# Down projections of three feed-forward layers: five seven-product pairs in place of four, and their shared sums folded earlier

## What is computed

```python
def _swiglu(t, w_gate, w_up, w_down):
    return (jax.nn.silu(t @ w_gate) * (t @ w_up)) @ w_down

for l in range(DEPTH):
    f = _swiglu(_rmsnorm(h, ffn1_pre_g[l]), ffn1_w_gate[l], ffn1_w_up[l], ffn1_w_down[l])
    h = h + 0.5 * _rmsnorm(f, ffn1_post_g[l])
    ...
    f = _swiglu(_rmsnorm(h, ffn2_pre_g[l]), ffn2_w_gate[l], ffn2_w_up[l], ffn2_w_down[l])
    h = h + 0.5 * _rmsnorm(f, ffn2_post_g[l])
```

## Time and profile before

| | |
|---|---|
| median of 3 runs (lowest, highest) | 1839.95 us (1839.8, 1840.28) |
| the profiled execution, its own time | 1839.19 us |
| its span, first to last instruction | 1837.2 us |
| TensorE busy | 1822.0 us (99%) |
| VectorE busy | 1372.0 us (75%) |
| ScalarE busy | 1115.8 us (61%) |
| GpSimd busy | 222.5 us (12%) |
| chain that ended last | PE 94%, DVE 4%, ACT 1%, issue 1% |
| HBM read | 330.91 MB, 181 GB/s over the span |
| granted TensorE clock, mean | 0.999 |

### The profile page before, as it was taken

How to read it: one execution, slowest core, us unless ns; L and a number is a source line. 1 busy time by engine, 2 the same in 40 slices (tenths; PEclk the granted TensorE clock), 3 DMA queues, 4 the chain that set the end, 5 groups by cost and what they waited for, 6 DMA issues and landing times.

```text
span 1837.2 us, 29020 instructions
## 1 busy us (share of the span) xinstructions
PE 1822.0 (99%) x10909; PEld 1625.8 (88%) x10909; DVE 1372.0 (75%) x2184; ACT 1115.8 (61%) x1924; POOL 222.5 (12%) x170
## 2 busy tenths in 40 slices
PE   9999999999999999999999999999999999999998
PEld 7888999998888878888999888887889998989997
DVE  7775757787787888878777778878768765768764
ACT  7664554556666566656555657665557654757653
POOL 0220001110033003300111102310002210001210
PEclk9999999999999999999999999999999999999999
DMA  8775575455576557655654548655747655537652
GB/s 247 216 217 183 172 194 163 146 154 186 172 226 185 182 166 225 191 177 160 192 173 142 194 147 230 185 176 168 218 138 218 188 196 155 169 115 205 202 191 103
DMA packets 436042, 333.88 MB, mean 182 GB/s; under 512 B 25402, under 2 KB 381504, under 8 KB 435904
## 3 DMA queue, kind: packets, MB, share of 16 engines
q1 hardware_dynamic: 435440, 331.57, 59.5%
q10 hardware_dynamic: 464, 0.47, 0.1%
HBM read 330.91 MB, written 1.05 MB: 181 GB/s over the span
## 4 chain that ended last, share of the span: by engine, by line
PE 94%; DVE 4%; ACT 1%; issue 1%; DMA 0%; SPq 0%; DVEq 0%; ACTq 0%
PE bank L1982 16%; PE bank L1959 14%; PE bank L1961 14%; PE bank L1960 14%; PE bank L1970 7%; PE bank L1984 7%; PE bank L1971 7%; PE bank L1972 7%; PE bank L1988 2%; DVE wlo L1250 1%; PE bank L1981 1%; DVE wsum L1383 1%; PE bank L2324 0%; PE bank L2390 0%; PE bank L2395 0%
## 5 line engine op out<-in xcount | busy, mean ns | idle before, releaser
L1250 DVE TENSOR_TENSOR wlo<-raw,whi 128x1024 fp32r<-128x1024 f32 (+3 forms) x634 | 748.7, 1189 | 224.5 <-ACT whi L676 217.8
L676 ACT ACTIVATE whi<-raw 128x1024 fp32r<-128x1024 f32 (+3 forms) x634 | 636.6, 1014 | 282.0 <-PE bank L1961 198.9
L1982 PE MATMUL bank<-U,whi 128*128 128x512 f32 x1280 | 439.1, 395 | 0.0
L1984 PE MATMUL bank<-U,wlo 128*128 128x256 f32 x1120 | 314.5, 281 | 0.0
L1970 PE MATMUL bank<-U,whi 128*128 128x256 f32 x1024 | 289.1, 282 | 0.0
L1972 PE MATMUL bank<-U,wlo 128*128 128x256 f32 x1024 | 285.9, 279 | 0.0
L1971 PE MATMUL bank<-U,whi 128*128 128x256 f32 x1024 | 285.9, 279 | 0.0
L1982 PEld LDWEIGHTS bank<-U,whi 128*128 128x128 f32 x1280 | 230.2, 188 | 42.5 <-issue 0.2
L1959 PE MATMUL bank<-whi,U 128*128 128x384 f32 (+2 forms) x592 | 218.9, 370 | 0.1
L1984 PEld LDWEIGHTS bank<-U,wlo 128*128 128x128 f32 x1120 | 210.1, 188 | 6.9
L1961 PE MATMUL bank<-wlo,U 128*128 128x384 f32 (+2 forms) x592 | 211.1, 357 | 0.0
(11 more groups left out here) (334 smaller groups left out, 2571.7 us busy)
## 6 DMA issues: line engine op xcount, KB each, us to landing
raw<-in_ffn_w_up SPq DMA_DIRECT2D x351, 256.0 KB, 3.5
raw<-in_ffn_w_down SPq DMA_DIRECT2D x264, 256.0 KB, 2.9
raw<-in_ffn_w_gate SPq DMA_DIRECT2D x175, 256.0 KB, 3.4
raw<-in_w_gate SPq DMA_DIRECT2D x128, 192.0 KB, 2.9
raw<-in_w_in SPq DMA_DIRECT2D x80, 256.0 KB, 3.4
raw<-in_a_w_in SPq DMA_DIRECT2D x48, 256.0 KB, 3.2
raw<-in_w_mem_kv SPq DMA_DIRECT2D x32, 256.0 KB, 3.2
raw<-in_w_out SPq DMA_DIRECT2D x32, 256.0 KB, 3.1
```

Of the source, the lines that this page charges most:

```text
L676: act.activation(whi[n % SLOTS][:, 0:w], unsplit(n, w), ACT.Copy).then_inc(hi_ready, 1)
L1250: dve.tensor_tensor(wlo[n % SLOTS][:, 0:w], unsplit(n, w), whi[n % SLOTS][:, 0:w].bitcast(F32), ALU.subtract).then_inc(lo_ready, 1)
L1982: ins = pe.matmul(dst, wh, u2[:, k, :], start=(k == 0), stop=(k == KT - 1))
L1984: pe.matmul(dst[:, 0:TOK], wl, uhi[:, k, :], start=False, stop=False)
```

## The change

- SEVEN becomes (1, 2, 3, 5, 6): the order of the pairs is 8 7 7 7 8 7 7 8 8, tail. One more pair of each of the three layers takes seven products.
- One of the four sums of activations (a21 + a22) is no longer kept in `ahi`, `alo`, but over the block a21 of `hhi`, `hlo`, which a seven-product pair does not read. ScalarE and GpSimd write it with an instruction of its own (128 columns, and 384 for the other three), after GpSimd has made `hlo` of that tile.
- The fold moves ahead of the last two ordinary pairs and takes nine steps: ScalarE copies bank 0 to `wsum`, VectorE forms the four shared sums between splits of the tail's chunks (bank 1 to the shared sum first, then banks 3 and 2 to that one, then bank 3 again), and adds them to banks 4 to 7 one after the other, each when TensorE has finished that bank's last matmul of the chunk before the tail (`rows_full`, new).

```diff
-SEVEN = (2, 4, 6, 8)
+SEVEN = (1, 2, 3, 5, 6)
...
-                    ahi, alo = sb("ahi", [P, NS, 4, P], F32R, m), sb("alo", [P, NS, 4, P], F32R, m)
+                    ahi, alo = sb("ahi", [P, NS, 3, P], F32R, m), sb("alo", [P, NS, 3, P], F32R, m)
...
         def _(pool):
...
-                        pool.wait_ge(ahi_done, x + 1)
-                        pool.tensor_tensor(alo[:, x % NS, :, :], asum[:, :, :], ahi[:, x % NS, :, :].bitcast(F32), ALU.subtract)\
-                            .then_inc(alo_done, 1)
+                        pool.wait_ge(asum_split, 4 * x + 2)
+                        pool.wait_ge(clo_done, wide(f, n - 2) + 1)
+                        pool.tensor_tensor(hlo[:, n - 2, ts[1]], asum[:, 0, :], hhi[:, n - 2, ts[1]].bitcast(F32), ALU.subtract)\
+                            .then_inc(asum_split, 1)
+                        pool.tensor_tensor(alo[:, x % NS, :, :], asum[:, 1:4, :], ahi[:, x % NS, :, :].bitcast(F32), ALU.subtract)\
+                            .then_inc(asum_split, 1)
...
         def _(act):
...
                         act.wait_ge(asum_done, 4 * x + 4)
-                        act.activation(ahi[:, x % NS, :, :], asum[:, :, :], ACT.Copy).then_inc(ahi_done, 1)
+                        act.wait_ge(clo_done, wide(f, n - 2) + 1)
+                        act.activation(hhi[:, n - 2, ts[1]], asum[:, 0, :], ACT.Copy).then_inc(asum_split, 1)
+                        act.activation(ahi[:, x % NS, :, :], asum[:, 1:4, :], ACT.Copy).then_inc(asum_split, 1)
...
+                if f:
+                    e = ck.seven[seven_of(f, SEVEN[-1])]
+                    split_to(e + 6)
+                    act.wait_ge(lo_ready, halves_done(e + 3))
+                    act.wait_ge(w_used, e + 1)
+                    act.activation(wsum[:, 0, :], bank[0][:, :], ACT.Copy).then_inc(folded, 1)
                 split_to(n0 + ffn_chunks(f) - TAIL - 1 + SLOTS)
...
             def fold(f):
...
-                split_to(e + 5)
-                dve.wait_ge(w_used, e + 1)
-                dve.wait_ge(lo_ready, halves_done(e + 3))
-                dve.tensor_copy(wsum[:, 0, :], bank[0][:, :]).then_inc(folded, 1)
-                split_to(e + 6)
-                dve.wait_ge(w_used, e + 2)
+                last = c_down[f][-1] - 3
+                split_to(e + 9)
+                dve.wait_ge(w_used, e + 4)
                 dve.wait_ge(folded, done + 1)
-                into_bank(4, 0)
-                split_to(e + 7)
-                dve.wait_ge(w_used, e + 3)
-                add_bank(2, 2, 0)
-                add_bank(1, 3, 0)
-                dve.wait_ge(w_used, e + 4)
+                add_bank(1, 1, 0)
+                split_to(e + 10)
+                dve.wait_ge(folded, done + 2)
+                add_bank(3, 3, 1)
+                add_bank(2, 2, 1)
+                split_to(e + 11)
                 dve.wait_ge(folded, done + 4)
-                add_bank(1, 1, 1)
-                dve.wait_ge(folded, done + 5)
-                into_bank(5, 1)
-                add_bank(2, 1, 2)
-                dve.wait_ge(folded, done + 7)
-                into_bank(6, 2)
-                add_bank(3, 3, 2)
-                dve.wait_ge(folded, done + 9)
-                into_bank(7, 3)
+                add_bank(1, 3, 2)
+                for n, x in enumerate((0, 3, 2, 1)):
+                    if n < 3:
+                        dve.wait_ge(rows_full, 3 * (f - 1) + n + 1)
+                    else:
+                        dve.wait_ge(w_used, last + 1)
+                        dve.wait_ge(folded, done + 5)
+                    into_bank(4 + n, x)
...
                 def hidden_sum(n):
-                    return ahi[:, x % NS, n, :], alo[:, x % NS, n, :]
+                    if n == 0:
+                        return hhi[:, even, ts[1]], hlo[:, even, ts[1]]
+                    return ahi[:, x % NS, n - 1, :], alo[:, x % NS, n - 1, :]
...
-                                ins = down_rows(c, t, nb, 4, hhi, hlo, k, k == 0, k == FT - TAIL - 3 and t + nb == 2)
+                                ins = down_rows(c, t, nb, 4, hhi, hlo, k, k == 0, k == FT - TAIL - 1)
+                                if k == FT - TAIL - 1 and t + nb < 2:
+                                    ins.then_inc(rows_full, 1)
...
-                    pe.wait_ge(folded, 10 * (f - 1) + (2, 6, 8, 10)[2 * t + nb])
+                    pe.wait_ge(folded, 9 * (f - 1) + 6 + 2 * t + nb)
```

More of the change, by code:

```diff
@@ L294, in program @@
             sem(n) for n in ("fx_rows", "f_step", "c_full", "c_ready", "c_pair"))
-        wsum_done, asum_done, ahi_done, alo_done, folded = (
-            sem(n) for n in ("wsum_done", "asum_done", "ahi_done", "alo_done", "folded"))
+        wsum_done, asum_done, asum_split, rows_full, folded = (
+            sem(n) for n in ("wsum_done", "asum_done", "asum_split", "rows_full", "folded"))
         feat_done, gt0_full, gate_done = sem("feat_done"), sem("gt0_full"), sem("gate_done")
@@ L1232, in weight_sums @@
                     dve.wait_ge(lo_ready, halves_done(ck.seven[x - 1] + 3))
-                    dve.wait_ge(folded, 10 * (x // NS))
+                    dve.wait_ge(folded, 9 * (x // NS))
                 at = ck.slot(e) * CW
@@ L1366, in hidden_sums @@
                 if x:
-                    dve.wait_ge(alo_done, x)
+                    dve.wait_ge(asum_split, 4 * x)
                 dve.tensor_tensor(asum[:, 0, :], a21, a22, ALU.add).then_inc(asum_done, 1)
@@ L1376, in fold @@
                 e = ck.seven[seven_of(f, SEVEN[-1])]
-                done = 10 * (f - 1)
+                done = 9 * (f - 1)
                 def into_bank(n, x):
@@ L2180, in seven_products @@
                 start_chunk(o)
-                product(4, hhi[:, odd, ts[0]], hlo[:, odd, ts[0]], o, half[1], False, stop)
-                pe.wait_ge(alo_done, x + 1)
-                product(5, *hidden_sum(3), o, half[0], False, stop).then_inc(w_used, 1)
+                product(4, hhi[:, odd, ts[0]], hlo[:, odd, ts[0]], o, half[1], False, False)
+                pe.wait_ge(asum_split, 4 * x + 4)
+                product(5, *hidden_sum(3), o, half[0], False, False).then_inc(w_used, 1)
                 start_chunk(sums)
@@ L2188, in seven_products @@
                 product(1, *hidden_sum(1), ends, half[0], start, stop)
-                product(6, hhi[:, odd, ts[1]], hlo[:, odd, ts[1]], ends, half[1], False, stop).then_inc(w_used, 1)
+                product(6, hhi[:, odd, ts[1]], hlo[:, odd, ts[1]], ends, half[1], False, False).then_inc(w_used, 1)
             def down_by_seven(f, b):
```

## The result

The changed kernel takes 1844.22 us (median of 20 runs, 1839.68 to 1847.96), the kernel before beside it 1839.83 us (20 runs, 1839.11 to 1841.33): ratio 1.0023, interval 1.0017 to 1.003. It is slower by 4.4 us. The forecast was 1839.4, with a range up to 1843.5. The single runs are spread over 8 us, those of before over 2.

What follows compares the result with a forecast made beforehand. TensorE, busy in 99% of the span, bounds the kernel; VectorE's queue sets the tail's start. Tail start 48.05 plus 8.4 gives 56.45 us a layer, 169.3 for three against 169.84, 0.5 less: 1839.4 us, range 1834.5 to 1843.5.

Steps and rivals of the forecast that it cites:

- (a): Gate tiles' end: pair 1's sums delay the last multiplication 1.55 us; VectorE begins pair 2 5.45 us after down projection's first matmul.
- the 0.42: Gate tiles: extra us for pair 1's sums, as one VectorE addition takes 1.11 instead of 0.69 beside GpSimd's instruction.
- the 0.8 more that the prediction kept open: Gate tiles: estimated extra us per layer if a sum waits for all 1.21 us of GpSimd's instruction; 1841.8 in all.
- (b): Pairs 2 and 3: VectorE's split of pair 3's o comes late, stalling TensorE 0.8 to 1.0 us.
- (c): Pairs 5 and 6: VectorE's split of pair 6's o comes late, stalling TensorE another 0.4 to 0.6 us.
- (d): Last splits: VectorE waits 1.2 us for the first tail chunk, splitting it 39.85 us after down projection's first matmul.
- (e): Tail splits and shared sums: 4.54 and 2.6 us of VectorE, late loads 0.15 us a layer, between 0 and 1.1.
- The rule of the page: Tail loads: HBM to SBUF bound by about 358 GB/s a core, chunks every 1.46 us, tail start 47.9 to 48.2.
- T0 + 48.05: Forecast tail start in each layer, in us from TensorE's first matmul of the down projection (T0).
- The covers: Gate tiles: extra ScalarE, GpSimd instructions and activation sums cost nothing; a failed cover costs its length three times, 1 to 3 us.
- the raw ring decides, slower: Tail: last four chunks' loads share DMA engines and land late; slower by over 3.7 us from 4.3; chance 0.14.
- Full gain: Down projections: with VectorE's queue 2.4 us shorter per layer TensorE never waits, 7.8 us less, 1832.1; chance 0.08.

Runs made afterwards that it cites:

- Experiment 2: Changed kernel with the loads of the tail's four chunks cut to 32 of each 512 columns, so mostly stale weights: 1834.75 us, ratio 0.9973.
- experiment 1: Changed kernel with four spaced seven-product pairs, SEVEN = (1, 2, 4, 6), in place of five, new fold kept: 1832.86 us, ratio 0.9962.
- experiment 3: Changed kernel with eight more matmuls into bank 0, result unread, ahead of each tail to fill TensorE's wait: 1841.45 us, ratio 1.001.
- experiment 8: Kernel of experiment 1 with three unused VectorE additions ahead of the addition to bank 4, making TensorE wait: 1838.28 us, ratio 0.9995.
- Experiments 6: Kernel before with only the activations' sum moved over the spent block of hhi and hlo, old pairs and fold: 1839.24 us, ratio 0.9997.
- experiment 7: Kernel before with the moved activations' sum and a fifth, spaced pair, SEVEN = (1, 2, 4, 6, 8), old fold: 1837.96 us, ratio 0.9989.
- experiments 4: Kernel of experiment 1 with five unused VectorE additions ahead of the addition to bank 4, making TensorE wait: 1846.48 us, ratio 1.0034.
- experiment 5: Changed kernel with four seven-product pairs standing together right ahead of the new fold, SEVEN = (3, 4, 5, 6): 1845.29 us, ratio 1.0042.

## Why the prediction was wrong

The mechanism was the one forecast: VectorE's queue, with the fold at its end, sets the start of the tail. The price of its last stretch was too low, and what TensorE's wait itself brings was not in it.

- **(a) Start of the queue: right.** VectorE begins pair 2 at T0 + 5.2, against 5.45. The last multiplication of the gate tiles comes at 607.26, against 605.35 in the earlier trace rows; T0 itself lies 0.66 later in this execution, so the delay is 1.25 us, against 1.55. One of pair 1's sums (L1250 at 601.99) takes 1.11 us beside GpSimd's instruction, the most in the trace, so the 0.42 stood, and the 0.8 more that the prediction kept open did not come: GpSimd's instruction (601.36 to 602.56) had 0.57 us left when the sum began.
- **(b), (c) Stalls at o: right in place, the first one 0.2 us smaller.** Forecast were 0.8 to 1.0 and 0.4 to 0.6 us. The idle times are 0.39 and 0.21; by the starts TensorE loses 0.66 and 0.48. (At pair 3 the starts are 0.79 apart instead of 0.23, and the next 0.33.) The queue was 0.25 us early, so o's split in pair 3 ends at T0 + 16.2 and not 16.46. Experiment 2 has these stalls alone: its stretch of 54.98 us is 1.2 longer than experiment 1's less the 0.68 of its three matmuls.
- **(d) First tail chunk: right.** T0 + 39.64 against 39.85, with its wait of 1.18 us against 1.2.
- **(e) The step that failed.** The term for the loads was 0.15 us a layer, between bounds of 0 and 1.1; it measured 1.8 (1.51 + 0.28) in ffn(1), 1.25 in ffn(2) and 1.55 in ffn(3). The upper bound took the longest landing of the earlier trace rows, 4.0 us, as if it held for any load. But those loads come in ones and twos, and the four chunks ask for 2.1 MB in 3.8 us. The trace of before holds better rows outside the 41 us of the earlier trace rows. Its eight loads from 862.0 us on (four of 256 KB, four of 172) are such a burst, and the last lands after 5.3 us; over the whole span the loads of this line land after 2.2, 3.2 and 7.5 us (shortest, median, longest). And 334 GB/s is not its busiest stretch: 346 to 348 us has 390.

```profile
L408 SPq DMA_DIRECT2D raw<-in_w_in x8: 328/434/507, 862.0 to 865.4; - x8
...
DMA to landing us min/median/max: 2.3/3.4/5.3
```

```profile
346.00:348.00 2.00, 2.00 (x13) 2.00 (x12) 1.44 (x2) 0.98 (x3) 0.11 (x1) 1.00 1.06 390
```

  The demand was worked out (460 GB/s), and also that at 334 GB/s the fourth chunk is 1.3 us late, of which the additions between the splits cover 1.0. But the working asked only about the fourth chunk, and had the chunks come evenly. By the high parts' ends (644.54, 647.28, 649.39, 650.80) against an undisturbed queue (a split at 644.57, 645.71, 647.5 and 649.8) the second is 1.6 us late, the third 1.9 and the fourth 1.0. Ahead of the second there is no addition to cover anything, and it lands 2.7 us behind the first. While its last half was under way (641.5 to 646.2) all the later ones were issued and up to six transfers were under way at once. Over three layers the tail starts are late by 3.8 us.
- **The rule of the page.** The Trainium skill, "DMA: Bandwidth & Descriptors", section "Where 436 GB/s comes from", has about 358 GB/s from HBM to SBUF for a core. The trace goes over it for 2 us (375 GB/s, in before 390) and stays under it over the whole burst (306). It is no ceiling here, and no rate to plan with either; the measurement decides.
- **What was not in the sum.** TensorE's wait of 2.1 to 2.6 us ahead of the tail lets its clock fall in part of the executions, 1.6 us in ffn(2) of the profiled one, an estimated 2 to 2.8 us in the median (experiment 3). The forecast put the sum together as if a stall cost only its length. With the tail at T0 + 48.05 it would probably have held: TensorE would have waited 1.3 us, and with waits of 1.0 to 1.9 only two of ten runs had a lower mean clock (experiment 8). That is argued and not shown.
- **The covers: right.** Experiments 6 and 7: no cost in the gate tiles.
- **The rivals.** What came true is *the raw ring decides, slower*, which had 0.14. It said that from a landing of 4.3 us on the change is slower, and 1844.5 at 4.6; the median of the eight was 4.6 and the result 1844.2. That this fits so closely is partly chance, since the clock's share was not in it. Its chance was set by the 4.0 us of the earlier trace rows. That was no evidence against it, since the stretch has no burst in it, and the rest of the trace of before, with the burst at 862 us and its landing of 5.3, spoke for it. The prediction had named landings after 4 us and more as a sign of being wrong, and this sign came. *Full gain*, 1832.1, is what experiment 1 comes near (1832.86), with four pairs.

Four spaced pairs under the new fold, 1832.86 us, are the best kernel here. A fifth costs VectorE 4.3 us a layer, for 0.68 us of TensorE, and in experiment 1 VectorE's idle time behind pair 6 is 1.24 + 0.87 + 0.33 + 0.42 = 2.9 us. In the old fold it paid: there the tail starts at T0 + 46.02 in experiment 7, before the fold is through.

What stays open: why the rate falls from 337 to 238 GB/s between 643 and 646 us, with up to six transfers under way, and is 375 later; and what decides whether the clock falls behind a wait, since 2.11 us had a fall behind it and 2.55 had none. No experiment took either apart. Spacing the tail's loads, or a fifth raw buffer, which would let the first of the four start earlier, was not tried.

## What to carry to other kernels

Cost a burst of loads by its own demand, and look for its bound in the whole trace: the longest landing of a stretch in which loads come in ones and twos is no upper bound for a burst, and another phase of the same kernel may hold such a burst already. The chunk to look at is the first one with no work between it and the one before, not the last. Put extra work for the second engine where it has idle time right behind, and keep the work that all wait for (here the fold) behind ordinary stretches; the same number of cheaper products can win 7 us or lose 5. And count a stall of TensorE of some 2 us as its length and, in part of the executions, over half as much again.

## What was not expected of the hardware

- **The clock behind a short wait.** In a stream of matmuls 0.23 us apart, waits of 2.1 to 2.8 us were followed, in four of eight cases in three profiled executions (changed kernel, experiments 4 and 5), by some 3.4 us at 1.2 GHz (granted clock 0.50), beginning 0.1 us after the wait in experiment 5 and 0.8 to 1 us after it in the others, at a price of 1.6 to 1.7 us. Behind the four waits of 1.0 to 1.9 us in the profiles of experiments 5 and 8 it didn't come; two of the ten runs of experiment 8 have a mean clock of 0.998. Filling the wait with matmuls whose result isn't used ended it (experiment 3).
- **Landing of a burst.** 256 KB took 2.9 us from issue to landing in the median of the earlier trace rows, and up to 5.9 when eight were issued in 3.8 us. In the three layers of the changed kernel's profile the fourth of the eight landed after 4.7 to 4.9 us, in experiment 3 after 3.9 to 5.2.
